# A decoder trunk on one core: the first two FFN units side by side, chunk by chunk, with early squares on GpSimd

## What is computed

```
x = x + 0.5 * swiglu(rmsnorm(x, g_norm[0, 0]), w_ffn_in[0, 0], w_ffn_out[0, 0])

rmsnorm(x, g) = x * rsqrt(mean(x * x) + EPS) * g
swiglu(h, w_in, w_out): g, u = split(h @ w_in); (silu(g) * u) @ w_out      # w_in is 1024 x 5632
```

## Time and profile before

| | us |
|---|---|
| median of 3 runs | 1243.33 (1243.26 to 1243.4) |
| profiled execution, its device time | 1244.23 |
| its span | 1242.4 |
| PE busy | 1232.9 |
| DVE busy | 725.6 |
| ACT busy | 580.1 |
| GpSimd (POOL) busy | 80.7 |

### The profile page before, as it was taken

The page is one execution under the profiler, slowest core; times in us unless marked ns, Lnnn a source line. Parts: engine busy times, 40 slices in busy tenths (PEclk is TensorE's granted clock), DMA queues, the critical chain, the costliest instruction groups (busy, mean ns, idle before and its releaser), DMA issues.

```text
span 1242.4 us, 21989 instructions
## 1 busy us (share of the span) xinstructions
PE 1232.9 (99%) x8849; PEld 1210.2 (97%) x8849; DVE 725.6 (58%) x1124; ACT 580.1 (47%) x930; POOL 80.7 (6%) x99
## 2 busy tenths in 40 slices
PE   9999999999999999999999999999999999999997
PEld 9999999989999999999998999999998999999997
DVE  6656554575777656554564565654467485655443
ACT  6534333454567444443445554533344464554332
POOL 0000000100332000000000000000020110000010
PEclk9999999999999999999999999999999999999998
DMA  8343334533354443334544744334578634443441
GB/s 341 136 164 140 117 128 160 207 134 133 128 163 151 154 166 135 137 117 143 194 154 143 255 139 165 124 117 142 179 273 327 263 136 158 146 145 117 140 140 42
DMA packets 35033, 200.40 MB, mean 161 GB/s; under 512 B 4058, under 2 KB 4442, under 8 KB 19746
## 3 DMA queue, kind: packets, MB, share of 16 engines
q1 hardware_dynamic: 32994, 192.27, 43.9%
q0 software_dynamic: 1984, 7.38, 1.9%
HBM read 193.06 MB, written 6.57 MB: 161 GB/s over the span
## 4 chain that ended last, share of the span: by engine, by line
PE 98%; DMA 0%; DVE 0%; ACT 0%; SPq 0%; issue 0%; DVEq 0%; ACTq 0%
PE bank L529 30%; PE bank L531 29%; PE bank L530 29%; PE bank L685 1%; PE bank L686 1%; PE bank L687 1%; PE bank L1029 1%; PE bank L689 1%; PE bank L688 1%; DMA xp<-xp_in 0%; PE bank L842 0%; PE bank L797 0%; PE bank L945 0%; PE bank L971 0%; PE bank L935 0%; PE bank L927 0%
## 5 line engine op out<-in xcount | busy, mean ns | idle before, releaser
L529 PE MATMUL bank<-h_hi,w_hi 128*128 128x320 f32 x1792 | 555.5, 310 | 0.8 <-DVE h_lo L1611 0.8
L531 PE MATMUL bank<-h_hi,w_lo 128*128 128x320 f32 x1792 | 553.7, 309 | 0.0
L530 PE MATMUL bank<-h_lo,w_hi 128*128 128x320 f32 x1792 | 553.7, 309 | 0.0
L1172 ACT ACTIVATE w_hi<-raw 128x1024 fp32r<-128x1024 f32 (+1 forms) x364 | 331.8, 958 | 443.1 <-PE bank L531 422.4
L1597 DVE TENSOR_TENSOR w_lo<-raw,w_hi 128x1024 fp32r<-128x1024 f32 (+1 forms) x364 | 388.4, 1107 | 134.0 <-ACT w_hi L1172 134.0
L529 PEld LDWEIGHTS bank<-h_hi,w_hi 128*128 128x128 f32 x1792 | 336.4, 188 | 2.3 <-DVE w_lo L1698 1.0
L530 PEld LDWEIGHTS bank<-h_lo,w_hi 128*128 128x128 f32 x1792 | 336.4, 188 | 0.1
L531 PEld LDWEIGHTS bank<-h_hi,w_lo 128*128 128x128 f32 x1792 | 336.4, 188 | 0.0
L529 PE MATMUL bank<-f_hi,w_hi 128*128 128x320 f32 x704 | 217.4, 309 | 0.0
L531 PE MATMUL bank<-f_hi,w_lo 128*128 128x320 f32 x704 | 217.4, 309 | 0.0
L530 PE MATMUL bank<-f_lo,w_hi 128*128 128x320 f32 x704 | 217.4, 309 | 0.0
(11 more groups left out here) (260 smaller groups left out, 759.8 us busy)
## 6 DMA issues: line engine op xcount, KB each, us to landing
raw<-w_in SPq DMA_DIRECT2D x86, 1024.0 KB, 4.8
raw<-w_out SPq DMA_DIRECT2D x64, 704.0 KB, 4.1
raw<-w_a SPq DMA_DIRECT2D x12, 1024.0 KB, 4.7
raw<-w_kv SPq DMA_DIRECT2D x8, 1024.0 KB, 4.7
raw<-w_oa SPq DMA_DIRECT2D x4, 1024.0 KB, 5.4
raw<-w_q SPq DMA_DIRECT2D x4, 1024.0 KB, 4.7
raw<-w_ob SPq DMA_DIRECT2D x4, 1024.0 KB, 11.8
raw<-kc_in SPq DMA_DIRECT2D x8, 512.0 KB, 4.6
```

What stands on the lines that cost most here:

```text
L529: pe.matmul(out, wh, mh, start=first, stop=False)
L530: pe.matmul(out, wh, ml, start=False, stop=False)
L531: return pe.matmul(out, wl, mh, start=False, stop=last)
L1172: sc.activation(w_hi[:, n_at % 2, part * w:part * w + w], raw[:, raw_of(n_at) % RAW, part * w:part * w + w], ACT.Copy).then_inc(hi_done, 1)
```

## The change

The first two units are stored interleaved in memory, chunk by chunk, and loaded so: for chunks 0 to 3 a transfer of 128 KB for each unit, for chunks 4 to 7 one of 256 KB for both; x comes in 6 pieces (chunks 0, 1, 2, 3, 4-5, 6-7), each ahead of its weights. That is 18 transfers for both units and x, where it was 8. The fourth unit is now issued ahead of the constants. ACT and DVE work in the same order, chunk by chunk: `h_hi`, then the chunk's weights of unit 0 and unit 1. TensorE multiplies 15 zeros without a wait and 1 after the first `h_hi`, then chunk by chunk for both units (12 products a chunk); for chunk 0 of unit 0 it does the two blocks' first pass, then their second, then their third. From chunk 5 on it finishes unit 0 first, then unit 1, with the square total ahead of the last chunk of unit 1 instead of within unit 2. Six of the eight squares and their running sum go to GpSimd (11 operations); ACT squares the last two chunks, DVE adds two. Unit 2 now goes to slot 0 of `w_hi`, which unit 0 must have left. On DVE the split of the fourth unit moves behind the reciprocal and the four scalings; on ACT behind the root.

```
-PIECES = ((0, 2), (2, 5), (5, 8))
+X_PIECES = ((0, 1), (1, 2), (2, 3), (3, 4), (4, 6), (6, 8))
+EACH = 4
@@ SP
+            def first_loads():
+                for k in range(KT):
+                    if X_PIECES[x_piece_of(k)][0] == k:
+                        load_x(x_piece_of(k))
+                    part = w_in[0, k // EACH][:, 512 * (k % EACH):512 * (k % EACH) + 512]
+                    if k < EACH:
+                        for u in range(2):
+                            sp.dma_start(raw_at(k)[:, 256 * u:256 * u + 256], part[:, 256 * u:256 * u + 256]).then_inc(
+                                loaded[0] if k == EACH - 1 and u else w01_each[k][u], 16)
+                    else:
+                        sp.dma_start(raw_at(k), part).then_inc(
+                            loaded[1] if k == KT - 1 else w01_both[k - EACH], 16)
@@ PE, first_units
-                zeros(9)
-                pe.wait_ge(lo_piece, 1)
-                zeros(2)
-                pe.wait_ge(s_x[0], 16)
+                zeros(15)
+                pe.wait_ge(hh_done, 1)
                 zeros(1)
+                pe.wait_ge(w01_hi, 1)
+                begin()
+                pe.wait_ge(w01_lo, 2)
+                both(1, 0)
+                for kt in range(1, EACH):
+                    pe.wait_ge(hl_done, kt + 1)
+                    for u in range(2):
+                        if kt == EACH - 1 and u:
+                            pe.wait_ge(lo_done, 1)
+                        else:
+                            pe.wait_ge(w01_lo, 2 * kt + u + 1)
+                        both(u, kt)
...
+                mm.then_inc(unit_done, 1)
+                both(1, 5)
+                both(1, 6)
+                total(0)
+                both(1, 7).then_inc(unit_done, 1)
                 pe.wait_ge(lo_first, 1)
+                chunk(bank[4][:, 0:T], 0, 0)
@@ ACT
+            for k in range(KT):
+                sc.wait_ge(s_x[x_piece_of(k)], 16)
+                h_split(k, N_A0)
+                if k < EACH:
+                    for u in range(2):
...
+                        sc.activation(split_piece(w_hi, k, u), raw_piece(k, u), ACT.Copy).then_inc(w01_hi, 1)
...
+            sc.activation(sq_room[:, 6:8, :], x[:, 6:8, :], ACT.Square).then_inc(sq_first, 1)
@@ DVE
+            for k in range(KT):
+                h_lo_of(k, N_A0, k + 1)
+                if k < EACH:
+                    for u in range(2):
+                        ve.wait_ge(w01_hi, 2 * k + u + 1)
+                        ve.tensor_tensor(split_piece(w_lo, k, u), raw_piece(k, u), split_piece(w_hi, k, u).bitcast(f32),
+                                         ALU.subtract).then_inc(lo_done if k == EACH - 1 and u else w01_lo, 1)
...
             def first_post():
+                ve.wait_ge(sq_first, 1)
+                chain.link(ve.tensor_tensor(sq_room[:, 6, :], sq_room[:, 6, :], sq_room[:, 7, :], ALU.add))
+                ve.wait_ge(sq_steps, 11)
+                ve.tensor_tensor(sqsum[:, :], sq_room[:, 0, :], sq_room[:, 6, :], ALU.add).then_inc(sum_first, 1)
+                split_half(2, 2, 0, lo_first)
+                split_half(2, 2, 1)
                 rms_of(0)
                 scaled(0, 0, 0, 0)
                 scaled(0, 1, 1, 0)
+                split_at(3)
@@ GpSimd, ahead of its wait for s_set 4
+            for m in range(6):
+                gp.wait_ge(s_x[x_piece_of(m)], 16)
+                gp.tensor_tensor(sq_room[:, m, :], x[:, m, :], x[:, m, :], ALU.mult).then_inc(sq_steps, 1)
+                if m:
+                    gp.wait_ge(sq_steps, 2 * m)
+                    gp.tensor_tensor(sq_room[:, 0, :], sq_room[:, 0, :], sq_room[:, m, :], ALU.add).then_inc(sq_steps, 1)
```

More of the change, by code:

```diff
@@ L602, in zeros, with begin @@
                         pe.matmul(bank[7][:, 0:128], work[:, 0:128], work[:, 128:256], start=True, stop=True)
-                zeros(9)
-                pe.wait_ge(lo_piece, 1)
-                zeros(2)
-                pe.wait_ge(s_x[0], 16)
-                zeros(1)
[L609 to L613, removed]
-                    pe.wait_ge(hl_done, kt + 1)
-                    for c in range(2):
-                        mm = chunk_part(bank[c][:, 0:T], 0, c, kt)
+                def begin():
+                    w = [slice(c * KT * 128, c * KT * 128 + 128) for c in range(2)]
+                    for c in range(2):
+                        pe.matmul(bank[c][:, 0:T], w_hi[:, 0, w[c]], h_hi[:, 0, :], start=True, stop=False)
+                    pe.wait_ge(hl_done, 1)
+                    for c in range(2):
+                        pe.matmul(bank[c][:, 0:T], w_hi[:, 0, w[c]], h_lo[:, 0, :], start=False, stop=False)
+                    pe.wait_ge(w01_lo, 1)
+                    for c in range(2):
+                        pe.matmul(bank[c][:, 0:T], w_lo[:, 0, w[c]], h_hi[:, 0, :], start=False, stop=False)
@@ new lines, in both @@
+                def both(u, kt):
+                    for c in range(2):
+                        mm = chunk_part(bank[2 * u + c][:, 0:T], u, c, kt)
+                    return mm
+                zeros(15)
+                pe.wait_ge(hh_done, 1)
+                zeros(1)
+                pe.wait_ge(w01_hi, 1)
[3 more added lines that the diff above has]
+                for kt in range(1, EACH):
+                    pe.wait_ge(hl_done, kt + 1)
+                    for u in range(2):
[4 more added lines that the diff above has]
+                        both(u, kt)
@@ L617, in first_units @@
+                pe.wait_ge(hl_done, 5)
+                pe.wait_ge(w01_lo, 2 * EACH)
+                both(0, 4)
+                both(1, 4)
+                for kt in range(5, KT):
+                    pe.wait_ge(hl_done, kt + 1)
+                    if kt < KT - 1:
+                        pe.wait_ge(w01_lo, 2 * EACH + kt - 4)
+                    else:
+                        pe.wait_ge(lo_done, 2)
+                    mm = both(0, kt)
                 mm.then_inc(unit_done, 1)
+                both(1, 5)
@@ L1243, in _ @@
             sc.activation(root[:, 0:1], epsc[:, :], ACT.Sqrt)
-            for q, (a, e) in enumerate(PIECES):
-                if q < len(PIECES) - 1:
-                    sc.wait_ge(w0_piece[q], 16)
-                else:
[L1248 to L1253, removed]
+            for k in range(KT):
[3 more added lines that the diff above has]
+                    for u in range(2):
+                        if k == EACH - 1 and u:
+                            sc.wait_ge(loaded[0], 16)
+                        else:
+                            sc.wait_ge(w01_each[k][u], 16)
+                        sc.activation(split_piece(w_hi, k, u), raw_piece(k, u), ACT.Copy).then_inc(w01_hi, 1)
+                else:
+                    if k < KT - 1:
+                        sc.wait_ge(w01_both[k - EACH], 16)
+                    else:
+                        sc.wait_ge(loaded[1], 16)
+                    ins = sc.activation(split_pieces(w_hi, k), raw_pieces(k), ACT.Copy)
+                    if k < KT - 1:
+                        ins.then_inc(w01_hi, 1)
+                    else:
+                        ins.then_inc(hi_done, 4)
+            sc.activation(sq_room[:, 6:8, :], x[:, 6:8, :], ACT.Square).then_inc(sq_first, 1)
             sc.wait_ge(s_set, 4)
@@ L1257, in first_post @@
                 half = PAIR // 2
[L1258 to L1265, removed]
+                sc.wait_ge(w2_half, 16)
+                sc.wait_ge(unit_done, 1)
+                sc.activation(w_hi[:, 0, 0:half], raw[:, 2, 0:half], ACT.Copy).then_inc(hi_done, 1)
+                sc.wait_ge(loaded[2], 16)
+                sc.activation(w_hi[:, 0, half:PAIR], raw[:, 2, half:PAIR], ACT.Copy).then_inc(hi_done, 1)
+                root_of(0)
                 split_at(3)
-                root_of(0)
                 hidden(0, 0, 0)
@@ L1704, in first_post @@
-            def first_post():
[L1705 to L1715, removed]
+            for k in range(KT):
[5 more added lines that the diff above has]
+                                         ALU.subtract).then_inc(lo_done if k == EACH - 1 and u else w01_lo, 1)
+                else:
+                    if k < KT - 1:
+                        ve.wait_ge(w01_hi, EACH + k + 1)
+                    else:
+                        ve.wait_ge(hi_done, 4)
+                    ve.tensor_tensor(split_pieces(w_lo, k), raw_pieces(k), split_pieces(w_hi, k).bitcast(f32),
+                                     ALU.subtract).then_inc(w01_lo if k < KT - 1 else lo_done, 1)
```

69 lines of the change are left out of this document (31 added, 38 removed).

## The result

The kernel after takes 1245.97 us (median, 1245.37 to 1246.86 in 20 runs), the kernel before beside it 1243.55 (1243.11 to 1244.41): ratio 1.0018, 95% interval [1.0012, 1.0024]. It is slower by 2.4 us, 0.2%; 1245.9 was forecast. The profiled executions took 1244.23 and 1245.93, a difference of 1.7 only, and of 1.3 in the span; the profile of before came from an execution 0.7 above its median. A second pair of profiles is under experiments 11 and 12.

The account below looks back on a forecast made before the run. PE, busy 1232.9 of 1242.4 us, was taken as the bound, so only its waits count: start -0.4, GpSimd contention and restarts +3.0, transfers and later units 0, giving +2.6 and a median of 1245.9 us; 8-in-10 range 1242.8 to 1248.2.

Parts of the forecast that it names:

- The sum: Whole kernel: -0.4 for the start and +3.0 for contention and restarts give +2.6 us.
- The start: PE's first product comes at 7.1 us, paced by 16 zeros, against before's effective 7.51: a gain of 0.4 us.
- lower bound of 6.5: PE's start: earliest first product, 6.5 us, if the clock rises right when the last merged load begins at 4.8.
- DVE and GpSimd: First two units: GpSimd's 11 operations alternate with DVE's splits and delay PE, net +2.2 to +2.8, taken +2.5 us.
- the floor by the work left: DVE's work left from 4.95 us: chunk 7 not ready before 20.3, PE asks at 17.7; net +2.2 us.
- the one by turns: Ten DVE/GpSimd turns of 1.02 us: chunk 3 ready about 15.6, PE 3.2 us late there; net +2.8 us.
- rival 1: First two units: contention stays hidden in DVE's slack of 3.5 us, PE bound by its zeros; 1242.9 us, chance 0.20.
- The hold: DVE beside GpSimd: each GpSimd operation holds DVE off for 0.69 us.
- Transfers: 18 loads for 8 at 346 KB/us land before the splits need them: cost 0, bounds 0 to 0.5 us.
- Rival 2: PE between 9 and 15 us: contention pauses make the clock fall, 2.5 us more lost; 1248.4 us, chance 0.13.
- Rival 3: Loads: small transfers halve the rate to 173 KB/us, chunk 7 lands at 22; 1248.6 us, chance 0.07.
- After the first two units: Third and fourth units' splits fit by 0.5 and 0.3 us, so no PE wait: taken 0, up to 0.5.

Follow-up runs that it names:

- experiments 11 and 12: Kernel before and kernel after, each run again unchanged for a second profile: 1243.39 and 1245.76 us for the profiled executions.
- experiment 7: Kernel after with 10 transfers instead of 18, squares back on ACT and DVE, the first half squared early behind chunk 3's split: 1243.58 us, ratio 0.9998.
- experiment 2: Kernel before with only the change's squares: six squares and five sums on GpSimd, two squares on ACT, one sum on DVE: 1247.93 us, ratio 1.0034.
- experiment 6: experiment 1 with the square of x chunks 0 to 3 and their first sum moved early, behind chunk 3's split: 1244.19 us, ratio 1.0001.
- experiment 10: experiment 6 with 11 GpSimd memsets of 128x640, which read nothing, placed where the kernel after has its GpSimd squares and sums: 1243.86 us, ratio 1.0003.
- experiment 3: Kernel after with 7 zeros in all instead of 16, squares still on GpSimd: 1246.05 us, ratio 1.0021.
- experiment 5: Kernel after with x and the first two units in 10 transfers instead of 18, squares still on GpSimd: 1246.32 us, ratio 1.0018.
- experiment 1: Kernel after with the squares as in before: ACT squares x in two operations after the splits, DVE sums, GpSimd does nothing there: 1245.71 us, ratio 1.0015.
- experiment 9: experiment 7 with the early square moved behind chunk 4's split on ACT and its first sum behind chunk 5's on DVE: 1244.37 us, ratio 1.0006.
- 4: experiment 1 (squares back on ACT and DVE) with 7 zeros in all instead of 16: 1245.17 us, ratio 1.0012.
- 8: experiment 7 (early square, ten transfers) with 7 zeros in all instead of 16: 1243.69 us, ratio 0.9998.

## Why the prediction was right

**The sum.** +2.6 us was forecast and +2.4 measured. That the median came out at 1245.97 for 1245.9 is luck to the last 0.2 us: before's median was 1243.55 and not the 1243.33 from which the sum started.

**The start.** 7.1 us was forecast, 7.31 and 7.49 measured, paced by the zeros as worked out; the spacing halved at 6.50 and 6.90 instead of 6.16 us. Against before's 7.51 that is worth 0.2 us and nothing, and not 0.4. The lower bound of 6.5 was too high: in the profile of experiment 7, with the same 16 zeros, the spacing halved at 4.1 and the first product stood at 6.18.

**DVE and GpSimd.** The mechanism held and decided the sign: experiments 2, 6 and 10 show it, with 4.2 us in the old order, some 2 in the new, and 0 if GpSimd doesn't read. The path was off in its middle. I had full alternation from 4.95 us on, chunk 3 ready at 15.6 to 15.9, and PE 3.2 us late there. It was ready at 12.5 (14.1 in the second profile), because GpSimd itself ran dry for x chunks 4 and 5, from 11.1 to 12.1 (11.5 to 11.9), and DVE caught up. Which of the two branches bound differs from profile to profile. In the first it is the floor by the work left: chunk 7's `w_lo`, forecast at 20.3, ended at 19.07, and PE took it up at 19.22. In the second it is the one by turns, a chunk later than forecast: GpSimd's last operation ends at 15.79, chunk 4's `w_lo`, the last that meets it, at 16.33, PE resumes for good at 16.48, and DVE, alone again, stays ahead of it. Experiments 3 and 5, with the squares on GpSimd as well, look like the second (17.03 and 16.79). With the start in them the branches gave +2.2 by the floor and +2.8 by turns; the last products stand 1.1 us apart in the first pair of profiles and 2.1 in the second. The two prices that the forecast averaged were thus both too high, the floor's by a factor of two. The slack of rival 1 was also taken as 3.5 us for both chunks, where 17.7 less 14.6 is 3.1.

The hold was sized right (1.08 for 0.42, 1.17 for 0.55). DVE's stretch over all its operations, by the groups of the kernel after less those of experiment 10, is 8 x 0.155 + 8 x 0.294 + 4 x 0.251 = 4.6 us, where I had 6.9: what falls into its waits for ACT costs nothing. By the rule that the prediction took from the Trainium skill (SBUF — State Buffer, Who interferes with whom), a hold of the whole instruction, it would have been more still (+4.5, an estimate); that section says "for the whole instruction" of DVE's 2-port mode. The measured hold decides, and it is less.

**Transfers: the step that failed.** I cost them at 0 by taking before's 346 KB/us. In 4 to 8 and 8 to 12 us they moved 281 and 263 GB/s, x chunks 4 and 5 came 2.9 us late (12.1, where that rate gives 9.2), chunk 7's `w_hi` ended at 16.8 for 13.6. SP's issues aren't the cause: the time from issue to landing grows from 2.6 us for the first transfer to 7.0 for the last of the 18, so they queue up behind one another. In the first profile a part of the wait before chunk 4 is theirs; in the second DVE has no pause from 6.4 us to there. It did not make the sum wrong because DVE was late anyway, and because the same gap let DVE catch up: two errors that partly cancel. Why they are slow stays open: experiment 5 doesn't blame their number alone, since ten transfers landed earlier at the end and later at the start.

**Rival 1** (contention hidden) is out. Its price looks too rosy as well: without contention the new order takes 1244.2 or 1243.9 (6 and 10), not 1242.9, though as a ratio to before (0.9997) that still lies within both intervals. In both profiles PE takes up chunk 4 late, at 14.21 and 14.33, behind x chunks 4 and 5, which land at 12.0 and 12.1; this takes the place of the old wait. **Rival 2**: apart from the waits, the product behind each and the square total, the products after 9 us are spaced 0.147 us in both profiles of the kernel after; the clock didn't fall there. **Rival 3**: the rate fell, by a fifth and by over a third of before's in the two stretches instead of half, and didn't bind alone.

**After the first two units** there is no wait of PE, as forecast.

**Open.** The last product of experiment 6 stands 0.1 to 0.4 us ahead of before's two (1231.42 against 1231.82 and 1231.56), its median 0.4 us behind (1244.19 against 1243.76, within the interval). Two draws go into each single profile: when the zeros speed up, and whether the clock falls ahead of the last six products, which it did in 6 (10.8 us behind the last product). How they fell in the timed runs is not shown. No experiment splits the 4.2 us of experiment 2 between the operations of GpSimd that cost most. No version tried beats before by more than the measurement can tell.

## What to carry to other kernels

Work moved to GpSimd is not free where it reads SBUF while DVE, itself reading two SBUF operands, is needed: look in the trace for the same pair of operations, one alone and one beside the other, and charge the difference to each turn. Operations that only write cost nothing here. When an engine in a full pipeline is slowed, work out the delay for every piece and not only for the first and the last: the piece that held PE was chunk 7 in one profile and chunk 4, the last one touched by GpSimd, in three others. And removing a wait without moving what stands behind it shows little; experiment 1 looked like a refutation until the next wait was moved too, and experiment 9 moved one and made another.

## What the hardware showed that was not expected

The moment at which PE's zeros go over from 0.21 to 0.11 us is a draw. PE starts at 1.20 us in every profile; in those with 16 zeros and no wait before the last of them the spacing halves at 6.5, 6.9, 5.2, 5.2, 5.6, 4.1, 7.3 and 4.8 us, and the first product follows at 6.2 to 7.7. In one profile with 7 zeros and pauses (experiment 3) the products stayed at 1.2 GHz until 10.4 us; in those of 4 and 8 they left it by 5.4. The prediction had this from the Trainium skill (TensorE: Matmul & The Clock Gate, Part 1: The HAM clock gate) as a statement that no run then showed; these do. A kernel whose start waits for data hardly sees the draw: in the two profiles of before the granted clock rises at 6.16 and 4.95 us, and the first product stands at 6.49 and 6.34. One whose start is paced by zeros does, by up to 1.5 us, but it costs time only where the start is what binds: in experiments 7 and 8 chunk 4 came at 14.4 from a start at 6.18 and from one at 4.57.

The fall at the end is a draw as well. In five of the fourteen profiles (before, after, 2, 5 and 6) the granted clock falls before the last of the kernel's six last products has begun, and the stretch behind the last 128x320 product takes 10.4 to 10.8 us; in eight it falls later, and the stretch takes 10.0. The fourteenth (10) has 10.5 with the later fall.

GpSimd's product of x with itself took 0.72 us alone (the first one in both profiles of the kernel after), less than the 0.88 of its sum of two tiles.
